# A second adaptive-norm block behind four norms' sums, taken from the odd projections, the masked phase and the scan

## What is computed

```
def adaln(cond, w, b):
    m = jax.nn.silu(cond) @ w + b
    return jnp.split(m[:, None, :], 6, axis=-1)

for i in range(DEPTH):
    sh1, sc1, g1, sh2, sc2, g2 = adaln(c, ada_w[i], ada_b[i])
    h_lat = modulate(rms_norm(x, norm_mix[i]), sh1, sc1)
    ...
    x = x + g1 * y_lat
    x = x + g2 * squared_relu_mlp(modulate(rms_norm(x, norm_mlp[i]), sh2, sc2), mlp_w1[i], mlp_w2[i])
```

## Time and profile before

| | us |
|---|---|
| median of 3 runs | 1828.66 |
| lowest and highest | 1824.95, 1829.68 |
| the profiled execution | 1824.08 |
| its span, first to last instruction | 1822.3 |
| PE busy | 1732.5 (95%) |
| DVE busy | 983.4 (54%) |
| ACT busy | 682.3 (37%) |
| POOL busy | 135.8 (7%) |

### The profile page before, as it was taken

One profiled execution on the slowest core, in us unless ns is written; L12 is line 12 of the kernel. 1 busy time (PEld: TensorE's weight loads), 2 busy tenths in 40 slices (PEclk: granted clock), 3 DMA queues, 4 the chain that ended last, 5 costly groups with the idle time before them and its releaser, 6 DMA issues.

```text
span 1822.3 us, 26395 instructions
## 1 busy us (share of the span) xinstructions
PE 1732.5 (95%) x10384; PEld 1363.6 (75%) x10384; DVE 983.4 (54%) x1788; ACT 682.3 (37%) x1238; POOL 135.8 (7%) x146
## 2 busy tenths in 40 slices
PE   5999999999999999998999999999889899999997
PEld 3775445578888887453689999777679799989997
DVE  3455873453434343345736666675478856554554
ACT  3433553241323132233635444543320066344443
POOL 1010000100000001033000000100115000200000
PEclk9999999999999999999999999999999999999999
DMA  9225783322222223243135444233130334344342
GB/s 398 81 93 231 261 300 133 139 92 93 93 93 93 93 93 131 95 186 130 56 111 202 174 174 184 83 139 139 47 139 2 126 117 175 140 183 167 146 161 83
DMA packets 21322, 254.00 MB, mean 139 GB/s; under 512 B 2256, under 2 KB 4560, under 8 KB 5584
## 3 DMA queue, kind: packets, MB, share of 16 engines
q1 hardware_dynamic: 18144, 242.51, 35.0%
q10 hardware_dynamic: 3056, 9.82, 1.5%
HBM read 251.26 MB, written 1.05 MB: 138 GB/s over the span
## 4 chain that ended last, share of the span: by engine, by line
PE 81%; DVE 10%; ACT 4%; issue 3%; DMA 1%; POOL 1%; DVEq 0%; POOLq 0%; SPq 0%; ACTq 0%
PE bank L548 17%; PE bank L550 16%; PE bank L549 16%; PE bank L505 14%; PE bank L987 4%; PE bank L605 3%; PE bank L680 2%; PE bank L706 2%; DVE w_lo L1698 2%; PE bank L688 2%; DMA weights<-in_ada 1%; ACT w_hi L1262 1%; DVE root L1574 1%; PE bank L659 1%; POOL root L2195 1%
## 5 line engine op out<-in xcount | busy, mean ns | idle before, releaser
L1698 DVE TENSOR_TENSOR w_lo<-weights,w_hi 128x1024 fp32r<-128x1024 f32 (+2 forms) x278 | 321.9, 1167 | 109.8 <-ACT w_hi L1262 107.0
L1262 ACT ACTIVATE w_hi<-weights 128x1024 fp32r<-128x1024 f32 (+2 forms) x278 | 278.9, 1011 | 231.8 <-PE bank L550 227.2
L548 PE MATMUL bank<-h_hi,w_hi 128*128 128x256 f32 (+1 forms) x960 | 315.0, 328 | 13.1 <-DVE w_lo L1698 6.7
L550 PE MATMUL bank<-h_hi,w_lo 128*128 128x256 f32 (+1 forms) x960 | 311.0, 324 | 0.0
L549 PE MATMUL bank<-h_lo,w_hi 128*128 128x256 f32 (+1 forms) x960 | 310.0, 323 | 0.0
L505 PE MATMUL bank<-slab,weights 128*128 128x256 f32 (+3 forms) x800 | 227.3, 439 | 2.1 <-DVEq L1814 1.2
L548 PEld LDWEIGHTS bank<-h_hi,w_hi 128*128 128x128 f32 x960 | 181.1, 189 | 35.1 <-issue 17.5
L505 PEld LDWEIGHTS bank<-slab,weights 128*128 128x128 f32 (+2 forms) x800 | 147.7, 187 | 76.9 <-issue 53.4
L550 PEld LDWEIGHTS bank<-h_hi,w_lo 128*128 128x128 f32 x960 | 180.6, 188 | 17.2
L549 PEld LDWEIGHTS bank<-h_lo,w_hi 128*128 128x128 f32 x960 | 181.1, 189 | 15.6
L548 PE MATMUL bank<-mlp_hidden_hi,w_hi 128*128 128x512 f32 (+1 forms) x512 | 174.7, 341 | 0.6 <-DVE w_lo L1698 0.6
(11 more groups left out here) (263 smaller groups left out, 2711.6 us busy)
## 6 DMA issues: line engine op xcount, KB each, us to landing
weights<-in_ada SPq DMA_DIRECT2D x36, 2048.0 KB, 8.1
weights<-in_mlp_up SPq DMA_DIRECT2D x16, 2048.0 KB, 8.0
weights<-in_mlp_down SPq DMA_DIRECT2D x16, 2048.0 KB, 8.2
weights<-in_ffn_in SPq DMA_DIRECT2D x11, 2048.0 KB, 8.2
weights<-in_in SPq DMA_DIRECT2D x8, 2048.0 KB, 8.1
weights<-in_gate SPq DMA_DIRECT2D x6, 2048.0 KB, 8.2
weights<-in_ffn_out SPq DMA_DIRECT2D x8, 1408.0 KB, 6.1
weights<-in_even_in SPq DMA_DIRECT2D x3, 2048.0 KB, 11.7
```

Of the source, the lines that this page charges most:

```text
L548: mm(b[:, 0:width], wh, hi(k), start=k == 0, stop=False)
L550: return mm(b[:, 0:width], wl, hi(k), start=False, stop=k == kc - 1)
L1262: A(split_part(w_hi, q), raw_part(q), ACT.Copy).then_inc(sem("w_hi_ready"), 1)
L1698: V.tensor_tensor(split_part(w_lo, q), raw_part(q), split_part(w_hi, q).bitcast(F32), ALU.subtract)\
```

## The change

`norm` gets a third setting of `fill`: with 2 it takes one adaptive-norm block between the sum's two matmuls, as before, and a second one behind the sum. Four norms use it: `mlp0`, `mix1`, `mlp1` and `mix2`. In each place four filler matmuls go. The four blocks for this are no longer taken in the `uq` projection, before `ukv`, in the masked phase, and in the last of the three scan steps that had one. The blocks keep their order; 36 are run as before.

```
-            def norm(name, width, fill=True, idle=0):
+            def norm(name, width, fill=1, idle=0):
@@
                 close(mm(b[:, 0:width], ones, sq[:, (DC - 1) % 2, 0:width], start=False, stop=True), t)
+                if fill == 2:
+                    ada_block()
@@
-            norm("mlp0", TOK)
-            mlp(0, TOK, (13, 4))
+            norm("mlp0", TOK, 2)
+            mlp(0, TOK, (9, 4))
-            norm("mix1", TOK)
+            norm("mix1", TOK, 2)
             ada_block()
@@
-                        before=h_ready("mix1") if i == 0 else None, idle=8 if i == 0 else 0)
+                        before=h_ready("mix1") if i == 0 else None, idle=4 if i == 0 else 0)
@@
-                    if i == 3:
-                        ada_block()
@@
             rope("kr", 0)
-            ada_block()
             w = take_block("ukv", 0)
@@
-            norm("mlp1", LAT, idle=4)
-            mlp(1, LAT, (8, 4))
-            norm("mix2", TOK, idle=6)
+            norm("mlp1", LAT, 2, 4)
+            mlp(1, LAT, (4, 4))
+            norm("mix2", TOK, 2, 6)
@@
-            split_linear("in2", [1], tag=lambda m: ("k", m), lead=True, idle=(12, 4),
+            split_linear("in2", [1], tag=lambda m: ("k", m), lead=True, idle=(8, 4),
@@
-                if n == 3:
-                    ada_block()
@@
-                if s < 3:
+                if s < 2:
                     ada_block()
```

## The result

| | before | after |
|---|---|---|
| median, us | 1827.7 (4 runs, 1824.95 to 1829.68) | 1865.3 (4 runs, 1862.83 to 1871.68) |
| the profiled execution, span | 1824.1, 1822.3 | 1862.8, 1861.0 |
| granted clock, mean | 0.987 | 0.974 |

The change makes the kernel 37.6 us slower. The ratio is 1.0212, with a 95% interval of 1.0191 to 1.0232. (Differences in this document are between medians; a ratio weighs all executions, so the two can differ by some us where the single times are spread.) The forecast was 35 us slower, at 1862, within 1848 to 1873.

The account below looks back on a forecast made before the run. TensorE was taken as the bound, busy 1732.5 of 1822.3 us. Transfers 33.3 plus clock 7.8 less 5.9 regained made 35.2 us slower: 1859.3 from the profiled execution, 1863.9 from the median, forecast 1862, range 1848 to 1873.

Parts of the forecast that it names:

- The transfers: At the four norms, later weight loads cost 17.3 + 13.8 + 0.8 + 1.4 = 33.3 us.
- The chain: At `mlp0` and `mlp1`, late load delays ACT's split, residual chunks 5 to 7, POOL's adds and TensorE's sum: 17.3 and 13.8 us.
- The clock: Slow clock after TensorE's idle time: 2.6 us each at `mlp0` and `mlp1`, 1.3 each at `mix1` and `mix2`, together 7.8.
- What came back: At the blocks' four old places, gains of 3.5 us in `uq`, 1.9 before `ukv`, 0 masked phase, 0.5 scan: together 5.9.
- The masked phase and the scan: Gain from the blocks leaving there: 0 us (bounds -1.9 and 1.9) and 0.5 us (bounds 0 and 1.9).
- The high end of the range: Whole kernel: 1873 us, named as the longer slow stretch counted from the median of the runs.
- Rival 1: Behind the gaps the full clock stays: 27.4 us slower, 1851.5, or 1856 from the median; chance 0.15.
- rival 2: Slow clock reaches the MLP's first matmuls, 5 us and more per long gap, 2.65 per short: about 8 more, 1870; chance 0.12.
- rival 3: At the MLP norms the sum doesn't wait for ACT's split; transfer hides behind root and reciprocal: 5.2 us slower; chance 0.04.
- the list of signs: New profile: later MLP load, ACT's DMA wait some 8 us, idle about 17 and 12 us, clock 0.50, `uq` wait gone.

Follow-up runs that it names:

- the second execution: The changed kernel run again with nothing edited: 1865.3 us, ratio 1.0207.
- The late release alone: Kernel before, no block moved; SP only holds both MLPs' first block back until the last product of the projection ahead ends: 1862.0 us, 33.1 slower.
- the split behind the root: Changed kernel with the early split at both MLP norms moved behind the root on ACT and the reciprocal on DVE: 1847.3 us, ratio 1.0099.
- the fillers: Changed kernel with 36 and 32 filler calls ahead of the sums at `mlp0` and `mlp1`: 1863.9 us, ratio 1.0188.
- `mlp1` alone: Kernel before with a second block only at `mlp1`, taken from the scan: 1845.2 us, 17.8 slower.
- a block in `ukv`'s wait: Kernel before with the adaptive-norm block that opens `ukv`'s second half moved into the 2.12 us wait in its first half: 1826.2 us, ratio 0.9989.
- the mixed norms alone: Kernel before with a second block only at `mix1` and `mix2`, taken from `uq` and the masked phase: 1831.7 us, ratio 1.0011.
- the two kept second blocks: Kernel before with second blocks at `mlp0` (loaded behind the MLP's first block) and `mix1`, taken from `uq` and `ukv`: 1821.3 us, ratio 0.9969.
- the loads the other way round: Changed kernel with the MLP's first block loaded ahead of the second adaptive-norm block at `mlp0` and `mlp1`: 1828.0 us, ratio 1.0009.
- `mlp0` alone: Kernel before with a second block only at `mlp0`, taken from ahead of `ukv`: 1843.0 us, 15.6 slower.

## Why the prediction was right, and where it was off

**The transfers: 33.3 forecast, 32.6 in the trace.** `mlp0` 17.3 against 17.1, `mlp1` 13.8 against 13.7, `mix1` 0.8 against 0.5 (in the second execution, less its clock, the same), `mix2` 1.4 against 1.3. The chain was as told: SP's issue at the end of the projection, a landing 8.0 us later, split, chunks 5 to 7, POOL, sum. The late release alone (33.1 us) and the split behind the root (18 us back) show that both links are causes, not companions: the first is what makes the load late, the second is what makes a late load stop TensorE.

**The clock: 7.8 forecast, 4.8 at these places.** For the long gaps 2.0 and 2.8 against 2.6 each, and 1.7 to 2.7 in the other traces that have these gaps; the fillers took them away. At the mixed norms 1.3 + 1.3 stood in the sum. The trace shows nothing at `mix2` behind a wait of 2.70, and at `mix1` nothing behind 3.49 in one execution and 2.8 behind 3.62 in the other. An expected value of 1.3 was fair for `mix1` (it is the mean of the nine traces above), but in a single trace it is nothing or 1.6 to 2.8. At `mix2` too the zero belongs to one execution: of the seven traces in which a wait there has grown, to 2.43 to 3.38 us, three show the clock falling at the first product or within 1.3 us of it (its matmuls took 0.63 for 0.40). The Trainium skill, "TensorE: Matmul & The Clock Gate" (section "What's actually happening"), says of the start of a kernel that the moment at which the clock rises varies from run to run of one kernel. Here, in the middle of one, whether it falls varies too, by 2.8 us at one place.

**What came back: 5.9 forecast, 6.0 in the trace.** `uq` 3.6 (3.5 forecast) and `ukv` 1.9 (1.9). The masked phase and the scan need care, since in the table above they add 1.6 instead of giving 0.5 back. The kernel with only the late release changes nothing there and yet adds 2.1 in the same stretch (from +37.5 at `mix2` to +39.6 at the norm `ffn`). Laid beside that kernel, the masked phase's block is gone at +1.9 and lost again by 2.1 at the next products, that is 0, as forecast; and the scan's place shifts by -0.5, as forecast. The step was right, but the table's line can't show it: over the thirteen traces this stretch adds between -1.8 us (`mlp1` alone) and +6.1 (fillers), whatever was changed. This drift goes with the granted clock. Between these two events it stood at 0.50 for 17.1 us before, 13.7 with `mlp1` alone, 20.5 in the kernel after and in that with the late release, and 30.7 with the fillers; half of the difference from 17.1 is what the stretch adds, within 0.7 us in eleven of the thirteen traces and within 1.6 in all.

**What was missed: 4.9 us in `ukv`, and the 2.1 us of drift.** No step of the forecast has them. The 4.9 are slow clock: the block there took 3.64 for 1.92 behind a wait of 2.12 that the kernel before has too. The rows I went by (nothing after 2.11, 2.65 after 4.80) made me treat short waits as harmless. One execution can't show that of a wait. The very wait of 2.11 us in `uq` was followed by the slow clock in two kernels that left it alone: with the late release (2.07 us there), and in the kernel before with a block in `ukv`'s wait (2.21 us). The row of the first; the block took 1.92 us before:

```profile
798.34 2.54 PE L605 MATMUL bank<-weights,cond 128*32 128x512 f32 x16 [2.07 <-DMA weights<-in_ada]
```

As to the stretch in `ukv`: in seven traces `uq` has given up its block and the wait of 2.12 us is left as it is, and five of them have the stretch (both of the changed kernel, the mixed norms alone, the split behind the root, the two kept second blocks); two don't (the loads the other way round, the fillers). Of the four with the wait in which `uq`'s block stands, none has it, and none of the three with a block inside the wait. Whether `ukv`'s own block has left seems not to matter: the mixed norms alone keep it and have the stretch, `mlp0` alone has lost it and has none. So in these traces it goes with the removal of `uq`'s block. But if five stretches fell by chance among these eleven traces, they would miss all of the four once in 22 times, the grouping was found after the fact, and why a block that ran 50 us ahead of the wait should matter was not found. It stays open.

**The sum.** 32.6 + 4.8 - 6.0 = 31.4 for what the steps name, where they said 35.2; to that come 4.9 in `ukv`, 2.1 of drift in masked phase and scan, and 0.3 of small shifts, which makes the 38.7 of the traces. So the transfers and what came back were right as steps, and that the total came so close was partly luck: 3.0 us of clock too much at the places named stand against 7 us of clock elsewhere that no step had. By these terms the clock cost 4.8 + 4.9 + 2.1 = 11.8 us more than before over the whole program, where 7.8 was forecast. (The high end of the range is not the sum that it names: 1828.7 + 35.2 + 8 is 1871.9, not 1873.) Rival 1 (27.4 slower, full clock) is refuted by 2.05 and 3.64 behind the gaps and by 4.7 us taken back at these places; rival 2 (5 us and more at each long gap) by the measured 2.0 and 2.8, though its other half, 2.65 at a short gap, is what `mix1` showed in one of two executions; rival 3 by the kernel with the late release, and it came true only when the split was moved.

Of the list of signs, all were seen: the issue at the end of L505, ACT's wait of 8 us behind it, idle times of 16.96 and 13.52 us (I had said about 17 and 12; the filler time that I took off at `mlp1` stood there before as well), clock 0.50, L605 without a wait behind L630, and no wait for `in_ada` in `uq`.

## What to carry to other kernels

When weights come through an in-order ring, adding work at one place means asking which later load now waits for a later release, and who stands behind that load on its engine; a block that took the place of filler on TensorE cost 16 to 18 us by the slot that it took. If something must go in there, put its load behind the one that is urgent, even if it then runs earlier or later than would be neat: with that at two norms, 37.6 us of loss became 0.6, not told apart from none. And where an in-order engine waits for a transfer, look at what it could have done first: moving the split behind the norm's root took about half of the loss back with the transfer as late as before.

## What the runs showed of the hardware that I had not expected

The same program at the same place, behind almost the same wait, ran at either clock: 1.97 us for eight filler instructions behind 3.49 us idle, 3.75 behind 3.62. In a third kernel they took 3.75 behind 3.48, so that the length of the wait does not decide it. A wait of 2.12 us was followed by full speed in one kernel and by 10.2 us at 0.50 in another (13.7 in its second execution), 4.9 to 6.2 us lost, more than the 2.0 lost behind an idle time of 17 us. The loss behind a gap is not in proportion to the gap.

Such a stretch is as large as 0.3% of this kernel. Where a kernel has ten runs or more, its single times spread over 6.6 to 15.5 us, and an effect of 4.7 us that the trace shows beyond doubt at two norms was 1.4 in the median. For a term below some 5 us, the trace around the place is the better measurement; for the sum of them, only many runs are.
